# The first transfers chained by their landings, the first two pieces cut smaller, and TensorE multiplying a cleared tile at the start of a decoder layer

## The chip, the cores and the metric

One Trainium2 chip, one of its cores. The number that counts is the device time of one execution in microseconds (us), as the median of the runs. Lower is better. The engines of the core are TensorE (PE in the profile, its weight loads apart as PEld), VectorE (DVE), ScalarE (ACT), GpSimd (POOL) and SyncE (SP), which issues almost all transfers.

## The reference

One layer of a decoder for 256 tokens of width 2048, all float32. Every `x @ w` below is a dense product, and the weights are far larger than what is held on the chip, so they are streamed.

```python
def swiglu(x, w_gate, w_up, w_down):
    return (jax.nn.silu(x @ w_gate) * (x @ w_up)) @ w_down
...
h = swiglu(rms_norm(x, ffn1_pre_g), ffn1_w_gate, ffn1_w_up, ffn1_w_down)   # 2048 -> 5632 -> 2048
x = x + 0.5 * rms_norm(h, ffn1_post_g)
u = rms_norm(x, mix_pre_g)
c_q, c_kv, k_rope, q_m, k_m, v_m = jnp.split(u @ w_in, cuts, axis=-1)
a = mla_attention(c_q, c_kv, k_rope, ...)
m = moba_attention(q_m, k_m, v_m)
y = jnp.concatenate([rms_norm(a, mla_out_g), rms_norm(m, moba_out_g)], axis=-1) @ w_out
x = x + rms_norm(y, mix_post_g)
h = swiglu(rms_norm(x, ffn2_pre_g), ffn2_w_gate, ffn2_w_up, ffn2_w_down)
x = x + 0.5 * rms_norm(h, ffn2_post_g)
```

Only the beginning of the first SwiGLU matters here: the product of the scaled x with the gate and up weights.

## The kernel before

**The stream.** The host lays all weights out as a stream of pieces, each `[128, 2048]` float32, 1 MB. In the gate-and-up stage a piece holds four chunks of 512 columns (256 gate and 256 up columns, for 128 rows of the contraction). Four pieces, 16 chunks, make the contraction over 2048 for one block of 256 hidden columns. SyncE loads the pieces in order into four slots of `raw` (piece n into slot n mod 4), and may load piece n only when the piece four earlier has been split (`raw_free`, a wait on `lo_ready`).

**The split.** The products are made from pairs of reduced-precision numbers. ScalarE rounds a piece to `w_hi`, and VectorE makes `w_lo = raw - w_hi` (`take_high`, `take_low`; two slots each, so `take_high` of piece n waits for `piece_used`, that TensorE is done with piece n - 2). TensorE then makes three products per chunk and token tile (`three_passes`): hi by hi, hi by lo, lo by hi. A piece is 4 chunks x 2 token tiles x 3 = 24 matmuls of 128x512.

**The left operand.** For the first stage the host gives x also turned (`x_turned`), and the transfer brings it to `xT` in four quads of four chunks, 512 KB each. `turn_high` (ScalarE, L406) multiplies a chunk by the gain of its rows and rounds it to `act_hi`. `turn_low` (VectorE, L711) makes `act_lo`. Each is one 128x256 instruction per chunk. TensorE waits for `act_ready` of each chunk, and for `lo_ready` of each piece.

**The gains** come as 70 rows of 128 numbers into `gain_in`. TensorE turns them with `ident` (L1406), and ScalarE copies the result to `gain`. Before TensorE can begin it waits for `consts_made`, `gains_landed` and `gains_kept`.

**The order at the start.** SyncE issues without a wait: the first half of piece 0, xT quad 0, the second half of piece 0, then piece 1, quad 1, piece 2, quad 2, piece 3, quad 3. Then piece 4, the first half of `rows` (x itself, 1 MB), piece 5, the second half of `rows`, piece 6, piece 7, a gain row and a table. ScalarE's order is: half 0 of piece 0, the gains, quad 0 (four chunks), half 1 of piece 0, piece 1, quad 1, piece 2, quad 2, quad 3, piece 3, the square of `rows` tile 0, piece 4, the square of tile 1, piece 5. VectorE follows in the same order, with piece 3 last of the first four. TensorE goes through the pieces in order.

```python
for n in range(RAW):
    if n:
        load(piece(n))
    sp.dma_start(xT[:, 4 * n:4 * n + 4, :], xT_in[:, 4 * n:4 * n + 4, :]).then_inc(xT_landed[n], 16)
```

Of the kernel before, what the change touches and what calls it, by code (L numbers as in the profile page):

```python
# [25 lines left out]
P = 128  # L26
# [14 lines left out]
RAW = 4  # L41
PIECE = 2048
EPS = 1e-6
# [8 lines left out]
GU1 = 0  # L52
# [56 lines left out]
def build_layer(nc, x, xT_in, stream, gains, post_gains, rope, out):  # L109
    ctx = ExitStack()  # L110
    with ctx:
# [14 lines left out]
        gain_in = sb("gain_in", [G_ROWS, P])  # L126
# [62 lines left out]
        xT_landed = [sem(f"xT_landed{k}") for k in range(4)]  # L189
# [8 lines left out]
        gains_turned = sem("gains_turned")  # L198
        gains_kept = sem("gains_kept")
# [21 lines left out]
        first_landed = sem("first_landed")  # L221
        first_hi_ready = sem("first_hi_ready")
        first_lo_ready = sem("first_lo_ready")
# [58 lines left out]
        def _(sp):  # L282
# [20 lines left out]

            sp.dma_start(raw[:, 0, 0:PIECE // 2], stream[0, :, 0:PIECE // 2]).then_inc(first_landed, 16)
            for n in range(RAW):
                if n:
                    load(piece(n))
                sp.dma_start(xT[:, 4 * n:4 * n + 4, :], xT_in[:, 4 * n:4 * n + 4, :]).then_inc(xT_landed[n], 16)
                if n == 0:
                    sp.dma_start(raw[:, 0, PIECE // 2:], stream[0, :, PIECE // 2:]).then_inc(raw_landed[0], 16)  # L310
# [27 lines left out]
        def _(pool):  # L338
            nc.gpsimd.memset(ident[:, :], 0.0)
            nc.gpsimd.memset(mask[:, :], 0.0)  # L340
# [49 lines left out]
        def _(act):  # L390
# [7 lines left out]
            def turn_high(turn, k, chunks=range(4)):  # L398

                if turn == 0:  # L400
                    act.wait_ge(xT_landed[k], 16)
                else:
                    act.wait_ge(quad_turned, 4 * (turn - 1) + k + 1)
                for j in chunks:
# [29 lines left out]
            def gate_up(stage, turn):  # L434


                turn_high(turn, 0)
# [223 lines left out]
            def mix_out():  # L661
# [37 lines left out]
        def _(dve):  # L699
# [5 lines left out]
            def turn_low(turn, k, chunks=range(4)):  # L705

                for j in chunks:
                    c = 4 * k + j
                    if j % 2 == 0:
# [347 lines left out]
            def scale_out(n, t):  # L1057
# [6 lines left out]
            dve.wait_ge(first_hi_ready, 1)  # L1064
            nc.vector.tensor_tensor(w_lo[:, 0, 0:PIECE // 2], raw[:, 0, 0:PIECE // 2], w_hi[:, 0, 0:PIECE // 2],
                                    ALU.subtract).then_inc(first_lo_ready, 1)
            dve.wait_ge(gains_kept, 1)
            turn_low(0, 0)
            dve.wait_ge(hi_ready, 1)
            nc.vector.tensor_tensor(w_lo[:, 0, PIECE // 2:], raw[:, 0, PIECE // 2:], w_hi[:, 0, PIECE // 2:],  # L1070
                                    ALU.subtract).then_inc(lo_ready, 1)
            take_low(piece(GU1 + 1))
            turn_low(0, 1)
# [19 lines left out]
        def _(pe):  # L1093
# [23 lines left out]
            def dense_piece(pc, i, blk, parity, width=BANK, n_turn=None):  # L1117

                halves = isinstance(pc.index, int) and pc.index == 0
                if halves:  # L1120
                    pe.wait_ge(first_lo_ready, 1)
                else:
                    pe.wait_ge(lo_ready, pc.index + 1)
# [3 lines left out]
                for j in range(4):  # L1127
                    c = 4 * i + j
                    if halves and j == 2:
# [259 lines left out]
            def mix_out():  # L1389
# [93 lines left out]
```

## Time and profile before

| | |
|---|---|
| median of 3 runs | 1875.18 us (1874.47 to 1875.34) |
| profiled execution, own time | 1875.26 us |
| its span, first to last instruction | 1873.4 us |
| TensorE matmul busy | 1847.7 us, 99% of the span |
| weight loads, VectorE, ScalarE | 1496.7, 934.6, 798.7 us |
| mean granted TensorE clock | 0.997 |
| first matmul of the product | 7.79 us after the span's start |

The span is what the trace shows; the execution's own time is 1.86 us longer. TensorE is busy nearly always, so the other engines' totals say little: what matters is when TensorE first starts, and each moment at which it stands.

### The profile page before, as it was taken

How to read it: one execution, taken by the hardware profiler on the slowest of the kernel's cores; microseconds unless marked ns; L12 is line 12 of the kernel's file. 1: busy time of each engine (PE TensorE's matmuls, PEld its weight loads, DVE VectorE, ACT ScalarE, POOL GpSimd, SP SyncE). 2: the span in 40 equal slices, each digit the busy share in tenths (PEclk: the TensorE clock that was granted, in tenths of full speed). 3: DMA queues.
4: the chain of work that ended last, by engine and by line, in shares of the span. 5: the costliest groups of instructions: out<-in, count | busy, mean ns of one | idle time of the engine just before them, and what ended most of it. 6: DMA issues, size and time to landing. Idle time of an engine off the chain costs nothing.

```text
span 1873.4 us, 21527 instructions
## 1 busy us (share of the span) xinstructions
PE 1847.7 (99%) x8233; PEld 1496.7 (80%) x8233; DVE 934.6 (50%) x857; ACT 798.7 (43%) x791; POOL 27.4 (1%) x59
## 2 busy tenths in 40 slices
PE   8999999999999999999999999999999999999997
PEld 6888888888878888788888878888888888788886
DVE  5444444444455554655577464444444444445545
ACT  6333433334444444543347345443333333444443
POOL 0000000000000000000000000000000000000000
PEclk9999999999999999999999999999999999999999
DMA  9454554545445545365441555555455554555552
GB/s 366 180 182 183 190 184 179 179 186 186 185 182 180 194 186 182 137 221 182 170 152 69 180 182 181 184 189 185 179 181 186 190 182 179 179 183 197 180 189 103
DMA packets 49063, 341.09 MB, mean 182 GB/s; under 512 B 5438, under 2 KB 5764, under 8 KB 9092
## 3 DMA queue, kind: packets, MB, share of 16 engines
q1 hardware_dynamic: 48944, 340.58, 50.2%
q8 instruction: 23, 0.38, 0.1%
q14 instruction: 12, 0.10, 0.0%
q10 hardware_dynamic: 84, 0.04, 0.0%
HBM read 338.50 MB, written 2.10 MB: 182 GB/s over the span
## 4 chain that ended last, share of the span: by engine, by line
PE 97%; DVE 1%; ACT 1%; issue 0%; DMA 0%; DVEq 0%; POOL 0%; ACTq 0%
PE banks L1191 26%; PE banks L1098 23%; PE banks L1096 23%; PE banks L1097 22%; PE banks L1161 1%; PE banks L1113 1%; DVE rows L735 0%; PE banks L1320 0%; PE banks L1321 0%; PE banks L1331 0%; DMA raw<-in_weights 0%; ACT w_hi L478 0%; DVE scaled L786 0%; PE banks L1227 0%; DVE w_lo L702 0%
## 5 line engine op out<-in xcount | busy, mean ns | idle before, releaser
L702 DVE TENSOR_TENSOR w_lo<-raw,w_hi 128x2048 fp32r<-128x2048 f32 (+3 forms) x229 | 515.1, 2249 | 671.2 <-ACT w_hi L395 671.2
L395 ACT ACTIVATE w_hi<-raw 128x2048 fp32r<-128x2048 f32 (+3 forms) x229 | 431.0, 1882 | 757.0 <-PE banks L1098 752.3
L1096 PE MATMUL banks<-w_hi,act_hi 128*128 128x512 f32 (+1 forms) x1728 | 686.1, 397 | 3.7 <-DVE act_lo L711 2.8
L1098 PE MATMUL banks<-w_hi,act_lo 128*128 128x512 f32 (+1 forms) x1728 | 683.7, 396 | 0.0
L1097 PE MATMUL banks<-w_lo,act_hi 128*128 128x512 f32 (+1 forms) x1728 | 678.4, 393 | 0.0
L1096 PEld LDWEIGHTS banks<-w_hi,act_hi 128*128 128x128 f32 x1728 | 325.4, 188 | 78.0 <-issue 3.9
L1097 PEld LDWEIGHTS banks<-w_lo,act_hi 128*128 128x128 f32 x1728 | 325.5, 188 | 77.4
L1098 PEld LDWEIGHTS banks<-w_hi,act_lo 128*128 128x128 f32 x1728 | 325.1, 188 | 77.5
L1191 PE MATMUL banks<-w_hi,hid_split 128*128 128x512 f32 x1408 | 386.1, 395 | 0.0
L775 DVE TENSOR_TENSOR w_lo<-raw,w_hi 128x2048 fp32r<-128x2048 f32 x88 | 201.6, 2291 | 236.3 <-ACT w_hi L478 236.3
L1191 PEld LDWEIGHTS banks<-w_hi,hid_split 128*128 128x128 f32 x1408 | 264.0, 188 | 65.5 <-DVE hid_split L778 0.5
L478 ACT ACTIVATE w_hi<-raw 128x2048 fp32r<-128x2048 f32 x88 | 168.6, 1916 | 269.2 <-PE banks L1191 255.4
L1191 PE MATMUL banks<-w_lo,hid_split 128*128 128x512 f32 x704 | 221.5, 396 | 0.0
L1191 PEld LDWEIGHTS banks<-w_lo,hid_split 128*128 128x128 f32 x704 | 132.2, 188 | 31.0
L778 DVE TENSOR_TENSOR hid_split<-hidT,hid_split 128x512 fp32r<-128x512 f32 x88 | 60.1, 683 | 0.0
L479 ACT CAST hid_split<-hidT 128x512 fp32r (+1 forms) x88 | 52.8, 600 | 0.0
L722 DVE SCALAR_TENSOR_TENSOR hid<-banks,rs,silu 128x256 f32<-128x256 f32 x88 | 38.2, 476 | 0.0
L425 ACT ACTIVATE silu<-banks,rs 128x256 f32<-128x256 f32 x88 | 36.1, 461 | 0.0
L368 POOL TENSOR_SCALAR var<-sumsq 128x1 f32<-128x1 f32 x20 | 8.1, 403 | 1542.3 <-ACT junk L415 1316.6
L431 ACT COPY hidT<-banks 128x512 f32 (+1 forms) x44 | 25.0, 567 | 6.6 <-PE banks L1161 6.6
L1161 PEld LDWEIGHTS banks<-ident,hid 128*128 128x128 f32 x176 | 21.7, 140 | 7.1 <-issue 1.4
L1161 PE MATMUL banks<-ident,hid 128*128 128x128 f32 x176 | 26.4, 272 | 0.5 <-DVE hid L722 0.5
(119 smaller groups left out, 606.5 us busy)
## 6 DMA issues: line engine op xcount, KB each, us to landing
raw<-in_weights SPq DMA_DIRECT2D x307, 1024.0 KB, 4.8
raw<-in_weights SPq DMA_DIRECT2D x6, 512.0 KB, 3.8
gain_row<-in_post_gains SPq DMA_DIRECT2D x3, 1024.0 KB, 6.9
raw<-in_weights SPq DMA_DIRECT2D x4, 768.0 KB, 4.1
raw<-in_weights SPq DMA_DIRECT2D x4, 640.0 KB, 3.8
xT<-in_x_turned SPq DMA_DIRECT2D x4, 512.0 KB, 10.2
rows<-in_x SPq DMA_DIRECT2D x2, 1024.0 KB, 13.8
out_rows<-rows SPq DMA_DIRECT2D x8, 256.0 KB, 2.8
```

The lines of the kernel that those rows point to most:

```text
L395: nc.scalar.activation(w_hi[:, pc.split, 0:width], raw[:, pc.slot, 0:width], ACT.Copy)\
L478: nc.scalar.activation(w_hi[:, pc.split, :], raw[:, pc.slot, :], ACT.Copy).then_inc(hi_ready, 1)
L479: nc.scalar.copy(hid_split[:, pc.split, 0], hidT[:, bass.ds(2 * n, 2), :]).then_inc(hid_hi_ready, 1)
L702: nc.vector.tensor_tensor(w_lo[:, pc.split, 0:width], raw[:, pc.slot, 0:width], w_hi[:, pc.split, 0:width], ALU.subtract).then_inc(lo_read ...
L722: nc.vector.scalar_tensor_tensor(out=hid[:, t, :], in0=result(parity, t)[:, FB:], scalar=rs[:, job, t:t + 1], in1=silu[:, t, :], op0=ALU.m ...
L775: nc.vector.tensor_tensor(w_lo[:, pc.split, :], raw[:, pc.slot, :], w_hi[:, pc.split, :], ALU.subtract)
L778: nc.vector.tensor_tensor(hid_split[:, pc.split, 1], hidT[:, bass.ds(2 * n, 2), :], hid_split[:, pc.split, 0], ALU.subtract).then_inc(lo_r ...
L1096: nc.tensor.matmul(out_ap, hi, rhs_hi, start=start, stop=False, skip_group_check=chain)
L1097: nc.tensor.matmul(out_ap, hi, rhs_lo, start=False, stop=False, skip_group_check=chain)
L1098: return nc.tensor.matmul(out_ap, lo, rhs_hi, start=False, stop=stop, skip_group_check=chain)
L1161: mm = nc.tensor.transpose(banks[:, 4, c * TOKENS + t * P:c * TOKENS + (t + 1) * P], hid[:, t, tile_of(c)], ident[:, :])
L1191: mm = nc.tensor.matmul(banks[:, b + n, :], lhs, rhs[:, j, quarter(n)], start=first and j == 0 and lhs is hi and rhs is rhs_hi, stop=True, ...
```

## The change

Transfers: piece 0 comes in four quarters (chunks) and the first xT quad in two pairs of chunks. The first four transfers are issued at once. Quarter 2 waits for quarter 0 to have landed, quarter 3 for the first pair, piece 1 for quarter 1, xT quad 1 for quarter 3, piece 2 for piece 1, and piece 3 for piece 2. What stands behind a waiting transfer on SyncE's queue waits with it.

Split: piece 0 is rounded and subtracted by quarters, each followed by its one chunk of x. Piece 1 goes by halves, each followed by two chunks of x. TensorE waits for each of these parts.

Gains: the host gives them turned, `[128, 70]`, and they land in `gain` directly. TensorE's turn of them, ScalarE's copy and both waits are gone.

TensorE: after GpSimd has cleared `mask` (now its first instruction of its own) and before it waits for the constants, it makes 10 matmuls of the cleared tile by itself into a bank that nothing reads.

```diff
+WARM = 10
...
-            sp.dma_start(raw[:, 0, 0:PIECE // 2], stream[0, :, 0:PIECE // 2]).then_inc(first_landed, 16)
-            for n in range(RAW):
-                if n:
-                    load(piece(n))
-                sp.dma_start(xT[:, 4 * n:4 * n + 4, :], xT_in[:, 4 * n:4 * n + 4, :]).then_inc(xT_landed[n], 16)
-                if n == 0:
-                    sp.dma_start(raw[:, 0, PIECE // 2:], stream[0, :, PIECE // 2:]).then_inc(raw_landed[0], 16)
+            def load_chunk(j):
+                sp.dma_start(raw[:, 0, quarter(j)], stream[0, :, quarter(j)]).then_inc(chunk_landed[j], 16)
+
+            for j in range(2):
+                load_chunk(j)
+                sp.dma_start(xT[:, 2 * j:2 * j + 2, :], xT_in[:, 2 * j:2 * j + 2, :]).then_inc(xT_pair_landed[j], 16)
+            sp.wait_ge(chunk_landed[0], 16)
+            load_chunk(2)
+            sp.wait_ge(xT_pair_landed[0], 16)
+            load_chunk(3)
+            for n in range(1, RAW):
+                if n == 1:
+                    sp.wait_ge(chunk_landed[1], 16)
+                else:
+                    sp.wait_ge(raw_landed[n - 1], 16)
+                load(piece(n))
+                if n == 1:
+                    sp.wait_ge(chunk_landed[3], 16)
+                sp.dma_start(xT[:, 4 * n:4 * n + 4, :], xT_in[:, 4 * n:4 * n + 4, :]).then_inc(xT_landed[n - 1], 16)
...
+            nc.gpsimd.memset(mask[:, :], 0.0).then_inc(mask_cleared, 1)
             nc.gpsimd.memset(ident[:, :], 0.0)
-            nc.gpsimd.memset(mask[:, :], 0.0)
...
                 if turn == 0:
-                    act.wait_ge(raw_landed[0], 16)
-                    nc.scalar.activation(w_hi[:, 0, PIECE // 2:], raw[:, 0, PIECE // 2:], ACT.Copy)\
-                      .then_inc(hi_ready, 1)
-                    take_high(piece(stage + 1))
-                turn_high(turn, 1)
+                    for j in range(4):
+                        act.wait_ge(chunk_landed[j], 16)
+                        nc.scalar.activation(w_hi[:, 0, quarter(j)], raw[:, 0, quarter(j)], ACT.Copy)\
+                          .then_inc(chunk_hi_ready if j < 3 else hi_ready, 1)
+                        if j == 0:
+                            act.wait_ge(gains_landed, 16)
+                        if j % 2 == 0:
+                            act.wait_ge(xT_pair_landed[j // 2], 16)
+                        turn_high(turn, 0, (j,))
+                    act.wait_ge(raw_landed[1], 16)
+                    for half in range(2):
+                        cols = slice(half * PIECE // 2, (half + 1) * PIECE // 2)
+                        nc.scalar.activation(w_hi[:, 1, cols], raw[:, 1, cols], ACT.Copy)\
+                          .then_inc(hi_ready if half else chunk_hi_ready, 1)
+                        if half == 0:
+                            turn_high(turn, 1, (0, 1))
+                else:
+                    turn_high(turn, 0)
+                turn_high(turn, 1, range(4) if turn else (2, 3))
...
-            act.dma_start(gain_in[:, :], gains).then_inc(gains_landed, 16)
-            act.wait_ge(first_landed, 16)
-            nc.scalar.activation(w_hi[:, 0, 0:PIECE // 2], raw[:, 0, 0:PIECE // 2], ACT.Copy)\
-              .then_inc(first_hi_ready, 1)
-            act.wait_ge(gains_turned, 1)
-            nc.scalar.copy(gain[:, :], banks[:, 7, 256:256 + G_ROWS]).then_inc(gains_kept, 1)
-            act.wait_ge(gains_kept, 1)
+            act.dma_start(gain[:, :], gains).then_inc(gains_landed, 16)
...
+            for j in range(4):
+                if j < 3:
+                    dve.wait_ge(chunk_hi_ready, j + 1)
+                else:
+                    dve.wait_ge(hi_ready, 1)
+                nc.vector.tensor_tensor(w_lo[:, 0, quarter(j)], raw[:, 0, quarter(j)], w_hi[:, 0, quarter(j)],
+                                        ALU.subtract).then_inc(chunk_lo_ready if j < 3 else lo_ready, 1)
+                turn_low(0, 0, (j,))
+            for half in range(2):
...
+                nc.vector.tensor_tensor(w_lo[:, 1, cols], raw[:, 1, cols], w_hi[:, 1, cols],
+                                        ALU.subtract).then_inc(lo_ready if half else chunk_lo_ready, 1)
+                turn_low(0, 1, (2 * half, 2 * half + 1))
...
+                    if early == 0 and j < 3:
+                        pe.wait_ge(chunk_lo_ready, j + 1)
+                    elif early == 0:
                         pe.wait_ge(lo_ready, 1)
+                    elif early == 1 and j == 0:
+                        pe.wait_ge(chunk_lo_ready, 4)
+                    elif early == 1 and j == 2:
+                        pe.wait_ge(lo_ready, 2)
...
+            pe.wait_ge(mask_cleared, 1)
+            for _ in range(WARM):
+                nc.tensor.matmul(banks[:, 5, 0:P], mask[:, 0:P], mask[:, 0:P], start=True, stop=True)
             pe.wait_ge(consts_made, 1)
-            pe.wait_ge(gains_landed, 16)
-            nc.tensor.transpose(banks[:, 7, 256:256 + G_ROWS], gain_in[:, :], ident[0:G_ROWS, 0:G_ROWS])\
-              .then_inc(gains_turned, 1)
-            pe.wait_ge(gains_kept, 1)
             gate_up(GU1, 0)
```

## Rows read from the trace of the kernel before

**Rows 1.** The page's first part: busy time, share of the span, instructions.

```profile
PE 1847.7 (99%) x8233; PEld 1496.7 (80%) x8233; DVE 934.6 (50%) x857; ACT 798.7 (43%) x791; POOL 27.4 (1%) x59
```

**Rows 2.** The page's chain that ended last, its shares by engine.

```profile
PE 97%; DVE 1%; ACT 1%; issue 0%; DMA 0%; DVEq 0%; POOL 0%; ACTq 0%
```

**Rows 3.** Timeline, 0 to 27 us: start, us, engine, line, count, [idle before <-releaser].

```profile
1.17 0.42 SPq L308 DMA_DIRECT2D xT<-in_x_turned  x1
...
4.82 1.06 ACT L678 ACTIVATE w_hi<-raw 128x1024 fp32r<-128x1024 f32 x1 [2.12 <-DMA raw<-in_weights]
...
5.91 1.23 DVE L1065 TENSOR_TENSOR w_lo<-raw,w_hi 128x1024 fp32r<-128x1024 f32 x1 [5.91 <-ACT w_hi L678]
6.13 1.70 ACT L406 ACTIVATE act_hi<-xT,gain 128x256 fp32r<-128x256 f32 x4
7.16 1.67 DVE L711 SCALAR_TENSOR_TENSOR act_lo<-xT,gain,act_hi 128x256 fp32r<-128x256 f32 x4
...
7.79 0.77 PE L1096 MATMUL banks<-w_hi,act_hi 128*128 128x512 f32 x1 [2.84 <-DVE act_lo L711]
...
10.45 1.92 ACT L395 ACTIVATE w_hi<-raw 128x2048 fp32r<-128x2048 f32 x1 [1.47 <-DMA raw<-in_weights]
...
12.40 2.29 DVE L702 TENSOR_TENSOR w_lo<-raw,w_hi 128x2048 fp32r<-128x2048 f32 x1 [2.16 <-ACT w_hi L395]
...
15.23 0.47 PE L1096 MATMUL banks<-w_hi,act_hi 128*128 128x512 f32 x1
...
19.24 1.71 ACT L406 ACTIVATE act_hi<-xT,gain 128x256 fp32r<-128x256 f32 x4 [0.33 <-DMA xT<-in_x_turned]
...
20.91 0.39 PE L1096 MATMUL banks<-w_hi,act_hi 128*128 128x512 f32 x1
...
21.17 1.92 ACT L395 ACTIVATE w_hi<-raw 128x2048 fp32r<-128x2048 f32 x1 [0.23 <-PE banks L1098]
...
23.12 2.29 DVE L702 TENSOR_TENSOR w_lo<-raw,w_hi 128x2048 fp32r<-128x2048 f32 x1 [0.32 <-ACT w_hi L395]
...
24.21 1.92 ACT L415 ACTIVATE junk<-rows 128x2048 bf16<-128x2048 f32 x1 [1.12 <-DMA rows<-in_x]
...
26.51 0.39 PE L1096 MATMUL banks<-w_hi,act_hi 128*128 128x512 f32 x1
```

**Rows 4.** DMA issues, 1.1 to 1.6 us: KB, us from issue to landing.

```profile
xT<-in_x_turned SPq DMA_DIRECT2D x1, 512.0 KB, 4.9
```

**Rows 5.** The page's DMA issues, whole span: count, KB, median us to landing.

```profile
raw<-in_weights SPq DMA_DIRECT2D x307, 1024.0 KB, 4.8
raw<-in_weights SPq DMA_DIRECT2D x6, 512.0 KB, 3.8
```

**Rows 6.** The tile raw, 60 to 400 us (59 loads of 1 MB).

```profile
DMA to landing us min/median/max: 4.6/4.8/6.0
```

**Rows 7.** Windows: us, busy (x) of PE, PEld, DVE, ACT, POOL, granted clock, DMA share, GB/s.

```profile
7.79:11.34 3.55, 3.55 (x8) 2.78 (x9) 2.27 (x4) 1.99 (x3) 0.00 (x0) 1.00 1.01 422
11.34:14.89 3.55, 3.55 (x16) 2.87 (x15) 2.49 (x2) 2.62 (x5) 0.00 (x0) 1.00 1.02 425
...
759.00:766.00 7.00, 4.34 (x20) 3.53 (x19) 5.58 (x10) 5.03 (x9) 0.81 (x2) 0.76 0.26 94
...
1111.10:1115.00 3.90, 3.89 (x11) 3.14 (x12) 3.90 (x6) 1.60 (x5) 0.00 (x0) 0.63 0.76 315
```

**Rows 8.** Timeline of PE, places inside the kernel where it stood.

```profile
762.60 2.82 PE L1113 MATMUL banks<-ident,rows 128*128 128x128 f32 x12 [1.88 <-DVE rows L735]
...
983.45 0.55 PE L1331 MATMUL banks<-ident,probs 128*128 128x128 f32 x3 [1.01 <-ACT probs L617]
983.84 0.39 PE L1341 MATMUL banks<-v,probsT 128*128 128x128 f32 x2
984.06 0.39 PE L1342 MATMUL banks<-v,probsT 128*128 128x128 f32 x2
...
1108.91 2.18 PE L1113 MATMUL banks<-ident,rows 128*128 128x128 f32 x12 [1.56 <-DVE rows L735]
```

More of the change, by code:

```diff
@@ L125, in build_layer @@
         mask = sb("mask", [P, 2 * P])
-        gain_in = sb("gain_in", [G_ROWS, P])
         gain = sb("gain", [P, G_ROWS])
@@ L186, in build_layer @@
         banks = ctx.enter_context(nc.psum_tensor("banks", [P, 8, BANK], F32))
-        xT_landed = [sem(f"xT_landed{k}") for k in range(4)]
+        xT_landed = [sem(f"xT_landed{k}") for k in range(1, 4)]
         rows_landed = [sem(f"rows_landed{t}") for t in range(TILES)]
@@ L197, in build_layer @@
         consts_made = sem("consts_made")
-        gains_turned = sem("gains_turned")
-        gains_kept = sem("gains_kept")
+        mask_cleared = sem("mask_cleared")
         hi_ready = sem("hi_ready")
@@ L220, in build_layer @@
         lat_ready = sem("lat_ready")
-        first_landed = sem("first_landed")
-        first_hi_ready = sem("first_hi_ready")
-        first_lo_ready = sem("first_lo_ready")
+        chunk_landed = [sem(f"chunk_landed{j}") for j in range(3)] + [raw_landed[0]]
+        xT_pair_landed = [sem(f"xT_pair_landed{j}") for j in range(2)]
+        chunk_hi_ready = sem("chunk_hi_ready")
+        chunk_lo_ready = sem("chunk_lo_ready")
         y_scaled = sem("y_scaled")
@@ L398, in turn_high @@
             def turn_high(turn, k, chunks=range(4)):
-                if turn == 0:
-                    act.wait_ge(xT_landed[k], 16)
-                else:
+                if turn:
                     act.wait_ge(quad_turned, 4 * (turn - 1) + k + 1)
+                elif k:
+                    act.wait_ge(xT_landed[k - 1], 16)
                 for j in chunks:
@@ L434, in gate_up @@
             def gate_up(stage, turn):
-                turn_high(turn, 0)
                 if turn == 0:
-                    act.wait_ge(raw_landed[0], 16)
-                    nc.scalar.activation(w_hi[:, 0, PIECE // 2:], raw[:, 0, PIECE // 2:], ACT.Copy)\
-                      .then_inc(hi_ready, 1)
-                    take_high(piece(stage + 1))
-                turn_high(turn, 1)
+                    for j in range(4):
[17 more added lines that the diff above has]
+                turn_high(turn, 1, range(4) if turn else (2, 3))
                 take_high(piece(stage + 2))
@@ L708, in turn_low @@
                     c = 4 * k + j
-                    if j % 2 == 0:
+                    if turn == 0 and k == 0:
+                        dve.wait_ge(act_hi_ready, j + 1)
+                    elif j % 2 == 0:
                         dve.wait_ge(act_hi_ready, DC * turn + c + 2)
@@ L1061, in scale_out @@
                                         ALU.mult).then_inc(y_scaled, 1)
[L1064 to L1073, printed above, removed]
+            for j in range(4):
[7 more added lines that the diff above has]
+            for half in range(2):
+                cols = slice(half * PIECE // 2, (half + 1) * PIECE // 2)
+                if half == 0:
+                    dve.wait_ge(chunk_hi_ready, 4)
+                else:
+                    dve.wait_ge(hi_ready, 2)
+                nc.vector.tensor_tensor(w_lo[:, 1, cols], raw[:, 1, cols], w_hi[:, 1, cols],
+                                        ALU.subtract).then_inc(lo_ready if half else chunk_lo_ready, 1)
+                turn_low(0, 1, (2 * half, 2 * half + 1))
             take_low(piece(GU1 + 2))
@@ L1117, in dense_piece @@
             def dense_piece(pc, i, blk, parity, width=BANK, n_turn=None):
[L1119 to L1122, printed above, removed]
+                early = pc.index if isinstance(pc.index, int) and pc.index < 2 else None
+                if early is None:
                     pe.wait_ge(lo_ready, pc.index + 1)
@@ L1128, in dense_piece @@
                     c = 4 * i + j
-                    if halves and j == 2:
+                    if early == 0 and j < 3:
+                        pe.wait_ge(chunk_lo_ready, j + 1)
+                    elif early == 0:
                         pe.wait_ge(lo_ready, 1)
+                    elif early == 1 and j == 0:
+                        pe.wait_ge(chunk_lo_ready, 4)
+                    elif early == 1 and j == 2:
+                        pe.wait_ge(lo_ready, 2)
                     if n_turn is not None:
@@ L1472 @@
         "weights": lay_out_weights(w),
-        "gains": np.concatenate(gains).reshape(G_ROWS, P),
+        "gains": np.ascontiguousarray(np.concatenate(gains).reshape(G_ROWS, P).T),
         "post_gains": np.concatenate([w["ffn1_post_g"], w["mix_post_g"], w["ffn2_post_g"]]),
```

## The prediction

> **What bounds the kernel now.** I read the page's busy times first, then the chain, then the timeline of the first 30 us. TensorE is busy 1847.7 of 1873.4 us [rows 1] and holds 97% of the chain that ended last [rows 2]. So a change at the start is worth exactly what it moves the point from which TensorE no longer stands; all after that point shifts with it. The reader should find that point first, and it isn't the first matmul.
>
> The start before, from [rows 3]: the first half of piece 0 lands at 4.8 us, ScalarE and VectorE work, and the first matmul starts at 7.79. Piece 1 starts at 15.23, piece 2 at 20.91, piece 3 at 26.51: 5.6 us apart, 24 matmuls at 0.233 us. The first 8 matmuls take 3.55 us and the next 16 take another 3.55 [rows 7], 0.44 against 0.22 each: TensorE begins at 1.2 GHz and rises to 2.4 GHz at about 11.3 (the clock column says 1.00 for both, so here the count has to be read, not the column). After 15.23 TensorE does not stand for a long time.
>
> But the supply is close behind. Piece 3 needs the last quad of xT, which lands at 19.24 (ScalarE stood for it [rows 3]). Then come, on ScalarE, 1.71 us for the quad and 1.92 for piece 3's w_hi, and on VectorE 2.29 for its w_lo, each started within 0.03 of the last: 5.95 us in all, so piece 3 could start at 19.24 + 5.95 = 25.2. It started at 26.51. Only 1.3 us of a gain in front of it can be kept, even if no transfer is later than now.
>
> **Transfers, the part that decides.** Before, nine transfers lie in the queue at once, and landings follow the bytes: 512 KB at 4.8, the next 512 KB at 1.17 + 4.9 = 6.07 [rows 3, 4], so 0.63 us per 256 KB; the 1 MB rows that land at 24.2 end 2 MB that follow the last quad, 2.5 us per MB [rows 3]. A transfer issued only when another has landed pays its full way: 4.8 us median for 1 MB, 3.8 for 512 KB [rows 5], bounds 4.6 and 6.0 [rows 6]. For 256 KB no row exists; the two medians continued give 3.3. Bounds: 2.9 (4.8 less 0.75 MB at 2.5 us per MB) and 3.8; I take 3.3, the nearer to the 512 KB row.
>
> The first four (1 MB) are issued as before: quarter 0 at about 4.2 (4.8 less 0.63), pair 0 at 4.8, quarter 1 at 5.45, pair 1 at 6.07. Quarter 2 is issued at 4.25 and lands at 7.55; quarter 3 at 4.85, lands 8.15. Piece 1 is issued at 5.5: 10.3 by the median, and by bytes it ends the same 2.5 MB as before, 10.45 [rows 3]; I take 10.45. Quad 1 follows it by 1.25: 11.7. Piece 2 is issued at 10.5 and lands at 15.3. Piece 3 is issued at 15.35 and lands at 20.15; quad 3, queued behind it, at 21.4. That is 2.15 later than the 19.24 of before. Everything queued behind on SyncE (piece 4, rows, piece 5) is as much later.
>
> By the Trainium skill, "DMA: Bandwidth & Descriptors", section "Anatomy of one DMA", a transfer has a fixed 2.0 us besides its bytes at 436 GB/s, mostly the receipt of the last byte, and its rules for kernel authors say to issue early and wait late; this speaks against the change. By its formula 1 MB would be an estimated 4.4 us instead of the measured 4.8, and the sum below 0.8 us smaller.
>
> **The first pieces.** A quarter of w_hi is 0.63 us (from 1.06 for half and 1.92 for a whole), a quarter of w_lo 0.70 (from 1.23 and 2.29), one chunk of x 0.42 to 0.5 on each engine [rows 3]. Chunk 0: w_hi 4.2 to 4.85, act_hi to 5.3, w_lo to 5.55, act_lo to 6.05, first matmul 6.1 instead of 7.79: 1.7 us earlier. The gains' own row is gone from this chain: no turn, no copy. They come now as 128 short rows instead of 70; should they land after 4.85, the first matmul is that much later, which the gap before piece 1 (below) covers up to 1 us. Chunks 1 to 3 are ready at 7.25, 9.35 and 10.5, a chunk takes 1.4 us at full clock, so piece 0 is done at 12.2.
>
> Piece 1: w_hi of its first half 10.45 to 11.5, w_lo to 12.75, act_hi of two chunks 11.7 to 12.55, act_lo of the first to 13.2. TensorE starts it at 13.25, after 1.05 us of standing, 2.0 earlier than before. The second half is ready at 15.35, needed at 16.05. Done at 18.9. Piece 2 (landed 15.3): w_hi to 17.2, w_lo to 19.5, act_lo to 19.95, start 20.0 after 1.1 us of standing; 0.9 earlier than before. Done at 25.65. Piece 3: 21.4 + 5.95 = 27.35, after 1.7 us of standing; 0.85 **later** than the 26.51 of before, and 0.9 with the slower first matmul after a stand (0.08, as at 15.23).
>
> Behind it: rows tile 0 lands 4.97 after quad 3 as before, 26.35; the square (1.92, and some 0.2 to read its sum, an estimate), w_hi and w_lo of piece 4 end at 32.65, while TensorE ends piece 3 at 33.0. That covers it by 0.35 us, whatever the landing, since both follow quad 3. From there nothing stands and the 0.9 stays to the end. The later stalls [rows 8] shift with it.
>
> **The cleared tile.** A float32 matmul of 128 columns shows as two records, 0.22 us at full clock from 983.84 to 984.06 [rows 8], so 0.44 at half: 10 cost 4.4 us. What covers them is the wait for chunk 0 until 6.1: begun before 1.7 us, which one memset ahead of them should allow, they cost nothing; if they ran past the cover, the first matmul would be later and again the gap before piece 1 would take it. Gain, if they raise the clock: 8 x 0.2 = 1.6 us in piece 0. But piece 1 waits for data until 13.25. Without any rise, piece 0 would end at 6.1 + 3.55 + 16 x 0.233 = 13.4; piece 1 starts 0.15 later, and piece 2's stand swallows that. So this part is worth 0 at the end, with bounds 0 and 1.6.
>
> **Sum.** Against the profiled execution's 1875.26: +0.9. The median shown is 0.08 below it, so 1875.18 + 0.9 = 1876.1 us.
>
> **Rivals.**
> Clock falls (0.22). Inside the kernel TensorE stood 1.88 us and 1.56 us [rows 8], and in both places the granted clock fell to 1.2 GHz for a while: a mean of 0.76 over 7 us and 0.63 over 3.9 us [rows 7], 3.4 and 2.9 us at half. After a stand of 1.01 the spacing stayed at full clock (two 128-column records in 0.22) [rows 8]. My stands are 1.05, 1.1 and 1.7. A fall before piece 1 or 2 is taken up by the next stand; one before piece 3 isn't: 8 matmuls at 0.2 more, +1.6, in all +2.5: 1877.7. The two rows with falls were among short transposes, not dense matmuls, which speaks against. The Trainium skill, "TensorE: Matmul & The Clock Gate", section "HAM oscillation", says the same of bursts parted by waits for data; the 1.56 row agrees. This is the rival on the other side of no change: with hops near 6.0 us (+2.4) it would be +4.9, and it decides from a hop of about 5.4 on.
> Waits cost nothing (0.22): the chained transfers land no later than now. For: the queue still holds a quad behind each piece. Then piece 3 starts at 25.2 + 0.08: 1.25 earlier, 1873.9.
> Hops much longer (0.05): slower by 3.75 needs quad 3 at 24.2, both hops at 6.2 us; 6.0 is the longest of 59. About 1879.
> Supply faster than now (0.05): bytes land 0.6 us or more earlier since fewer transfers share the engines, all gains at the start kept: start 1.7, clock 1.6 and the stand from 14.89 to 15.23 [rows 3, 7] of 0.35, 3.65 and so 1871.5 at the very most; about 1872.5 for most of it.
> The forecast itself (0.46), with hops of 4.6 to 5.2: own range 1875.6 to 1876.9.
>
> **Numbers.** A measurement of this kernel can tell about 0.2%, 3.75 us, from no change. The largest gain is 3.65, so faster by more has 0.02; slower by more needs the long hops, or a fallen clock with middling ones: 0.07; same 0.91. The range 1873.8 to 1878.2 takes in the forecast, the fallen clock and the free waits, and leaves out the two ends and a part of the middle ones.
>
> **What would show it.** Right: first matmul near 6.1; three stands of TensorE before pieces 1, 2 and 3, released by VectorE; piece 2 and 3 landing 4.8 after issue; quad 3 near 21.4; DMA share with holes where it was 1.0; piece 3 starting at 27.3. Half-clock spacing after the last stand shows the first rival. Wrong: if quad 3 lands before 20.6, the sum turns to a gain; if the spacing in piece 0 is 0.44 the tile did nothing, and the end shouldn't move by it.

## The result

The changed kernel takes 1881.73 us (median of 7 runs, 1878.82 to 1883.17), the kernel before 1874.73 (7 runs, 1874.21 to 1875.34). The ratio is 1.0033, with a 95% interval of 1.0023 to 1.0043: slower by 0.33%, 7.0 us between the two medians. The forecast was no change, 1876.1 us, with a range up to 1878.2. The runs of the changed kernel also scatter over 4.4 us where those of before scatter over 1.1. One execution in all that follows took 9123.58 us, one of the seven of the run with quad 1 behind piece 1's landing; it is left out of that run's ratio.

The page of the changed kernel, its busy times and its chain by engine. Beside [rows 1] and [rows 2]: TensorE is 6.7 us longer busy, of which 4.6 us are the matmuls of the cleared tile, and transfers now have 1% of the chain.

```profile
PE 1854.4 (99%) x8252; PEld 1501.7 (80%) x8252; DVE 935.3 (50%) x860; ACT 799.2 (43%) x793; POOL 27.5 (1%) x59
...
PE 96%; DVE 1%; DMA 1%; ACT 1%; issue 0%; SPq 0%; DVEq 0%; POOL 0%; ACTq 0%
```

The timeline of the changed kernel, columns as in [rows 3], put in order of time. SPq L290 issues pieces, SPq L322 quads of xT.

```profile
1.09 4.64 PE L1438 MATMUL banks<-mask 128*128 128x128 f32 x20 [1.09 <-POOL mask L351]
...
5.93 0.33 SPq L290 DMA_DIRECT2D raw<-in_weights  x1
6.52 0.76 PE L1124 MATMUL banks<-w_hi,act_hi 128*128 128x512 f32 x1 [0.79 <-DVE act_lo L732]
...
9.73 0.33 SPq L322 DMA_DIRECT2D xT<-in_x_turned  x1
...
12.21 0.33 SPq L290 DMA_DIRECT2D raw<-in_weights  x1
12.22 1.06 ACT L462 ACTIVATE w_hi<-raw 128x1024 fp32r<-128x1024 f32 x1 [1.45 <-DMA raw<-in_weights]
...
14.60 0.91 ACT L418 ACTIVATE act_hi<-xT,gain 128x256 fp32r<-128x256 f32 x2 [1.33 <-DMA xT<-in_x_turned]
16.17 0.47 PE L1124 MATMUL banks<-w_hi,act_hi 128*128 128x512 f32 x1 [2.27 <-DVE act_lo L732]
19.64 1.91 ACT L407 ACTIVATE w_hi<-raw 128x2048 fp32r<-128x2048 f32 x1 [2.39 <-DMA raw<-in_weights]
...
24.42 0.47 PE L1124 MATMUL banks<-w_hi,act_hi 128*128 128x512 f32 x1 [0.87 <-DVE act_lo L732]
26.36 1.71 ACT L418 ACTIVATE act_hi<-xT,gain 128x256 fp32r<-128x256 f32 x4 [3.21 <-DMA xT<-in_x_turned]
27.98 1.90 ACT L407 ACTIVATE w_hi<-raw 128x2048 fp32r<-128x2048 f32 x1
29.91 2.29 DVE L721 TENSOR_TENSOR w_lo<-raw,w_hi 128x2048 fp32r<-128x2048 f32 x1 [0.93 <-ACT w_hi L407]
32.26 0.50 PE L1124 MATMUL banks<-w_hi,act_hi 128*128 128x512 f32 x1 [2.00 <-DVE w_lo L721]
```

Read it from the bottom. Piece 3 starts at 32.26, where it started at 26.51 [rows 3]: 5.75 us later. Above it stands the chain of quad 3: landed at 26.34, then 1.7 + 1.9 + 2.3 us of work, 5.9 in all. So quad 3's landing is what moved, from 19.24 to 26.34. Further up are the hops (a hop is the time of one transfer from its issue to its landing): piece 1 issued at 5.93 and landed at 12.2 (6.3 us), piece 2 issued at 12.21 and landed at 19.6 (7.4 us), and quad 1 issued at 9.73 only, for it waits for quarter 3, and landed at 14.6 (4.9 us).

The windows of the changed kernel, columns as in [rows 7]; the last one lies in piece 3.

```profile
6.00:8.00 2.00, 1.48 (x4) 1.22 (x5) 1.46 (x3) 0.97 (x2) 0.00 (x0) 1.00 0.62 179
...
12.00:14.00 2.00, 1.91 (x9) 1.20 (x7) 0.69 (x1) 1.06 (x1) 0.00 (x0) 1.00 0.88 225
...
18.00:19.60 1.60, 1.60 (x5) 1.28 (x4) 0.50 (x2) 0.00 (x0) 0.00 (x0) 0.50 0.07 31
...
33.80:37.20 3.40, 3.40 (x10) 2.66 (x9) 2.03 (x1) 1.34 (x1) 0.46 (x1) 0.50 1.00 424
```

The kernel before, the same three stretches of the start (the last two columns are the share of the transfer engines and GB/s).

```profile
6.00:8.00 2.00, 0.21 (x1) 0.24 (x2) 1.98 (x4) 1.78 (x5) 0.00 (x0) 1.00 0.98 352
...
12.00:14.00 2.00, 2.00 (x11) 1.59 (x10) 1.60 (x1) 1.96 (x5) 0.00 (x0) 1.00 0.99 412
...
18.00:19.60 1.60, 1.60 (x9) 1.28 (x8) 1.60 (x2) 1.27 (x4) 0.00 (x0) 1.00 1.06 438
```

There are the holes: 179 GB/s instead of 352, 225 instead of 412, and before piece 2 lands 1.6 us at 31 GB/s and a share of 0.07. That is one of the 16 transfer engines: the trace has a landing event for each engine's part of piece 2, and fifteen of them come between 16.65 and 17.28, the sixteenth at 19.62. All that time SyncE holds back the next piece. And the granted clock falls to half after the stand of 2.0 us, 1.5 us after piece 3 has started: 3.4 us at 0.50, some 8 matmuls at 0.43 instead of 0.233, 1.55 us that nothing takes up. 5.75 + 1.55 = 7.3 us. The copies of the hidden columns bear it out: from 53 to 526 us each of them stands 7.4 us later than before, so nothing more is lost there and the steady part keeps its pace. After 1156 us they stand 6.5 us later, as much as the span grew: of the two later falls of the clock in [rows 7], the one near 1111 us does not occur in this execution.

### The profile page after: what moved, and what is told of

It is laid out like the page before. It is cut to its first block, busy times and chain, and to the rows that moved or that the text cites. A ratio compares the mean times of both kernels' runs of the same rounds, so it can differ in the third digit from the quotient of the medians.

```text
span 1879.9 us, 21574 instructions
## 1 busy us (share of the span) xinstructions
PE 1854.4 (99%) x8252; PEld 1501.7 (80%) x8252; DVE 935.3 (50%) x860; ACT 799.2 (43%) x793; POOL 27.5 (1%) x59
## 4 chain that ended last, share of the span: by engine, by line
PE 96%; DVE 1%; DMA 1%; ACT 1%; issue 0%; SPq 0%; DVEq 0%; POOL 0%; ACTq 0%
PE banks L1223 25%; PE banks L1126 22%; PE banks L1124 22%; PE banks L1125 22%; PE banks L1193 1%; DMA raw<-in_weights 1%; PE banks L1141 1%; DVE rows L756 0%; DMA xT<-in_x_turned 0%; DVE w_lo L721 0%; PE banks L1352 0%; PE banks L1353 0%; PE banks L1363 0%; ACT w_hi L503 0%; ACT w_hi L407 0%
```

## The experiments

Times are medians, each beside the kernel before on the same chip (1874.94 to 1875.01 in every group). "Quad 3" is the moment at which its first act_hi starts after standing for the transfer; it is read from the one profiled execution, while the time is the median of all. A shorter way to say where a run stands: piece 3 starts 5.9 us after quad 3, unless TensorE is later.

**All waits out.**

```diff
-            sp.wait_ge(chunk_landed[0], 16)
             load_chunk(2)
-            sp.wait_ge(xT_pair_landed[0], 16)
             load_chunk(3)
             for n in range(1, RAW):
-                if n == 1:
-                    sp.wait_ge(chunk_landed[1], 16)
-                else:
-                    sp.wait_ge(raw_landed[n - 1], 16)
                 load(piece(n))
-                if n == 1:
-                    sp.wait_ge(chunk_landed[3], 16)
```

> The changed kernel with all of SyncE's waits for landings at the start taken out; sizes and order of the transfers stay. Theory A (the chained waits make each transfer pay its whole way, which the queue otherwise hides): quad 3 of xT lands near 19.3 us instead of 26.3, the stand before piece 3 shrinks from 2.0 us to under 0.5, the time is 1872.5 to 1874.5. Theory B (the small first transfers are what is slow: they put back everything behind them): quad 3 still lands after 22 us, time over 1876.5. Theory C (the clock that falls after TensorE's stands is most of the loss): only 1.5 us less than the changed kernel, about 1880.

1874.62 us, ratio to the kernel before 0.9999 (0.9990 to 1.0008). The whole loss, 7.1 us, is the waits'. The timeline of this run:

```profile
6.37 0.48 PE L1116 MATMUL banks<-w_hi,act_hi 128*128 128x512 f32 x1 [0.64 <-DVE act_lo L724]
...
20.85 1.71 ACT L410 ACTIVATE act_hi<-xT,gain 128x256 fp32r<-128x256 f32 x4 [1.47 <-DMA xT<-in_x_turned]
...
26.74 0.50 PE L1116 MATMUL banks<-w_hi,act_hi 128*128 128x512 f32 x1 [0.25 <-DVE w_lo L713]
```

Its window from 6 to 8 us, where before has 352 GB/s and the changed kernel 179:

```profile
6.00:8.00 2.00, 1.63 (x7) 1.37 (x8) 1.31 (x3) 0.85 (x2) 0.00 (x0) 1.00 0.90 271
```

TensorE begins 1.4 us earlier than before and here at full clock, and piece 3 still starts at 26.74: quad 3 landed at 20.8, 1.6 later than before, though nothing waits. Theory A is right in that the waits make the loss, but its figures (quad 3 near 19.3, at most 1874.5 us) are missed by little: something else eats the rest of the gain. Note piece 1, which lands at 12.07 here, hardly earlier than the 12.2 of the changed kernel.

**Only the early waits.** The same edit for pieces 2 and 3 alone.

> The changed kernel without the waits of piece 2 for piece 1 and of piece 3 for piece 2; the four waits on quarters and the first pair stay. Theory A: the two long hops (7.4 and 4.8 us from issue to landing) carry most of the loss; piece 2 and 3 land by bytes behind piece 1, which landed at 12.2 against 10.4, so quad 3 lands at about 21 and the time is 1875 to 1877. Theory B: over 1878.

1878.59 us (1875.07 to 1880.72), 1.0016 (1.0007 to 1.0025); quad 3 at 23.83. Theory A's figure of 1875 to 1877 was too low. By the medians, taking out the last two waits gains 3.1 us and the early waits carry 4.0 (this run's own times scatter over 5.7 us). The reason shows in the queue: quad 1 still waits for quarter 3, so it and all behind it are issued from 9.81 on only.

**No cleared tile.** The loop of ten matmuls taken out.

> The changed kernel without the ten matmuls of the cleared tile. In the changed kernel the first real matmuls are 0.43 us apart all the same, until 3.4 us after they begin. Theory A: no difference to the changed kernel beyond 1 us, 1879 to 1883, since a later piece waits for its transfer anyway. Theory C: if the cleared tile does change the clock's course (where it falls and rises), the time moves by 1.5 us or more.

1880.84 us (1877.63 to 1882.08), 1.0027 (1.0016 to 1.0038), quad 3 at 25.66. The interval overlaps that of the changed kernel. No worth of the tile shows at the end, as the forecast had it.

**The kernel before with only the two late waits.**

```diff
                 if n:
+                    if n > 1:
+                        sp.wait_ge(raw_landed[n - 1], 16)
                     load(piece(n))
```

> The kernel before with only two waits added: piece 2 is issued when piece 1 has landed, piece 3 when piece 2 has. Theory A: piece 1 lands at 10.4 as before, two hops of 4.8 to 7.4 follow, quad 3 lands at 21.4 to 25, time 1876 to 1881. Theory B: within 1 us of the kernel before, 1874 to 1876.

1876.01 us (1875.28 to 1876.89), 1.0006 (0.9997 to 1.0015). The timeline of this run:

```profile
10.42 1.91 ACT L397 ACTIVATE w_hi<-raw 128x2048 fp32r<-128x2048 f32 x1 [1.50 <-DMA raw<-in_weights]
...
15.35 0.33 SPq L290 DMA_DIRECT2D raw<-in_weights  x1
...
21.82 1.71 ACT L408 ACTIVATE act_hi<-xT,gain 128x256 fp32r<-128x256 f32 x4 [2.87 <-DMA xT<-in_x_turned]
...
27.71 0.50 PE L1098 MATMUL banks<-w_hi,act_hi 128*128 128x512 f32 x1 [1.06 <-DVE w_lo L704]
```

This is the forecast's own chain, almost to the tenth: piece 1 at 10.4, one hop of 4.9, quad 3 at 21.8 (forecast 21.4), piece 3 at 27.71 (27.35), +1.0 us (+0.9). The arithmetic of the late hops was right; what goes before them in the changed kernel was not.

**Large first transfers, no waits.** Half, quad and half as before; ScalarE's waits adapted, the work by quarters kept.

```diff
-            for j in range(2):
-                load_chunk(j)
-                sp.dma_start(xT[:, 2 * j:2 * j + 2, :], ...)
-            load_chunk(2)
-            load_chunk(3)
+            sp.dma_start(raw[:, 0, 0:PIECE // 2], ...).then_inc(chunk_landed[1], 16)
+            sp.dma_start(xT[:, 0:4, :], ...).then_inc(xT_pair_landed[0], 16)
+            sp.dma_start(raw[:, 0, PIECE // 2:], ...).then_inc(chunk_landed[3], 16)
```

> The changed kernel without SyncE's waits and with the first transfers in the sizes of before (half, quad, half), while ScalarE, VectorE and TensorE still go by quarters; the gains come turned, the cleared tile stays. Without waits but with small transfers piece 1 landed at 12.1 and quad 3 at 20.8 us, against 10.45 and 19.24 before. Theory B2 (the 256 KB transfers with their 2 KB rows move the same bytes more slowly, some 1.6 us in all): piece 1 at 10.4, quad 3 near 19.3, piece 3 starts near 25.3, time 1873 to 1874. Theory G (the gains, now 128 rows of 280 bytes instead of 70 of 512, are what is slow): piece 1 still near 12, quad 3 near 20.8, time 1874.6 as without waits.

1874.52 us, 0.9997 (0.9988 to 1.0006). Piece 1 at 11.28, quad 3 at 20.59, against 12.07 and 20.85 with the small ones. Neither theory's figures hold: the sizes account for 0.8 us at piece 1 and little at quad 3.

**Gains in 512-byte rows, no waits, small transfers.** The host pads the turned gains to `[128, 128]`.

> The changed kernel without SyncE's waits, with the turned gains padded by the host to 128 rows of 512 bytes; the small transfers stay. Theory G: piece 1 lands near 10.5, quad 3 near 19.3, time about 1873.5. Theory B2: as without waits, piece 1 near 12.1, quad 3 near 20.8, time within 0.5 us of 1874.6.

1870.52 us, 0.9973 (0.9962 to 0.9985): lower than either theory, with quad 3 at 20.11 and piece 3 at 26.01. Only 0.7 us lie there. The rest lies in the steady part, 22.75 us per block of hidden columns instead of 22.84: the padding had also shifted every tile that is allocated later. The two things had to be parted (below).

**Quad 1 not waiting.** The changed kernel without the one wait on `chunk_landed[3]`.

> The changed kernel with one wait taken out: quad 1 of xT no longer waits for quarter 3 but is issued right behind piece 1. Theory Q (piece 2's hop of 7.4 us is long because quad 1, issued at 9.7, is still in flight when piece 2 is issued at 12.2): piece 2's hop falls to about 5, quad 3 lands 1.5 to 2.5 us earlier than 26.3, time 1.5 to 2.5 us less than the changed kernel's, 1879 to 1880. Theory S (a single lagging transfer engine makes the hop long, whatever lies behind it): quad 3 near 25.5 to 26.5, time 1880.5 to 1882.5.

1879.07 us, 1.0023 (1.0013 to 1.0033), 2.7 below the changed kernel. The timeline of this run:

```profile
12.37 0.33 SPq L290 DMA_DIRECT2D raw<-in_weights  x1
...
17.09 1.91 ACT L405 ACTIVATE w_hi<-raw 128x2048 fp32r<-128x2048 f32 x1 [0.82 <-DMA raw<-in_weights]
...
23.58 1.71 ACT L416 ACTIVATE act_hi<-xT,gain 128x256 fp32r<-128x256 f32 x4 [2.97 <-DMA xT<-in_x_turned]
...
29.47 0.50 PE L1122 MATMUL banks<-w_hi,act_hi 128*128 128x512 f32 x1 [1.75 <-DVE w_lo L719]
```

Piece 2's hop is 4.7 instead of 7.4, quad 3 2.8 us earlier and the time 2.7 us less: theory Q, by a little more than it said. In the four traces that keep this wait, the chain and the small transfers (the changed kernel, the one without the cleared tile, the one with padded gains, the shifted one) the hop of piece 2 is 6.5 to 7.4. So this one wait makes the hop long.

**The kernel before with the whole chain of waits**, large transfers kept.

```diff
                 if n:
+                    sp.wait_ge(xT_landed[0] if n == 1 else raw_landed[n - 1], 16)
                     load(piece(n))
+                if n == 1:
+                    sp.wait_ge(raw_landed[0], 16)
                 sp.dma_start(xT[:, 4 * n:4 * n + 4, :], ...)
                 if n == 0:
+                    sp.wait_ge(first_landed, 16)
                     sp.dma_start(raw[:, 0, PIECE // 2:], ...)
```

> The kernel before, large first transfers and all, with the whole chain of waits: second half for first half, piece 1 for quad 0, quad 1 for the second half, piece 2 for piece 1, piece 3 for piece 2. Theory A (waits alone, whatever the sizes): hops of 4.8 to 5: second half lands near 8.9, piece 1 at 11 to 12, quad 1 near 13, piece 2 at 16.5, quad 3 at 22.8 to 23.5, time 1877 to 1878. Theory B2 (waits and small transfers each have a part): this one stays 3 us or more below the changed kernel's 1881.7. Theory A2 (the early waits are what cost, sizes do nothing): quad 3 at 25 or later, time 1879 to 1882.

1879.06 us (1877.51 to 1880.47), 1.0021 (1.0012 to 1.0030). The timeline of this run:

```profile
6.22 0.33 SPq L290 DMA_DIRECT2D raw<-in_weights  x1
...
13.62 1.92 ACT L399 ACTIVATE w_hi<-raw 128x2048 fp32r<-128x2048 f32 x1 [3.87 <-DMA raw<-in_weights]
...
25.20 1.71 ACT L410 ACTIVATE act_hi<-xT,gain 128x256 fp32r<-128x256 f32 x4 [3.18 <-DMA xT<-in_x_turned]
```

So large transfers do not save a chain: piece 1 takes 7.4 us here. Landing and time are both where A2 put them, at the low end. Quad 1 waits too, but lands only 1.3 us after piece 1 (14.87), and piece 2's hop behind it is 4.9. B2's mark, 3 us or more below the changed kernel, is missed by little at 2.7, so a small part of the sizes isn't excluded.

**Place in memory.** The kernel before with one unused tile (32 bytes per partition) behind `gain`, nothing else.

```diff
         gain = sb("gain", [P, G_ROWS])
+        sb("shift_by", [P, 8])
```

> The kernel before with one unused tile of 32 bytes per partition allocated behind gain: everything allocated later, act_hi, act_lo and hid_split among it, then starts at a multiple of 64 bytes instead of 32 past one. Nothing else differs. Theory P (place in memory: the 0.09 us per block of hidden columns by which the run with padded gains was quicker in its steady part comes from this shift, which the padding brought about): 22.75 instead of 22.84 us per block, time near 1871. Theory G2 (it is the gains' rows in some way): no change, 1875.

1843.20 us (1841.81 to 1844.54), 0.9833 (0.9819 to 0.9846). The place does it, and by far more than either theory gave.

Gains in 512-byte rows without waits, with the later tiles put back to their old place:

> The changed kernel without SyncE's waits, gains in 128 rows of 512 bytes, and the same unused tile of 32 bytes, which here puts the later tiles back to 32 past a multiple of 64, as in the kernel before. It compares with the run without waits (1874.6, quad 3 at 20.85) in the gains' rows alone. Theory P: 22.84 us per block; the time is 1873.5 to 1874.6, by what the rows move quad 3 (20.1 to 20.8). Theory G2: near 1870.5 as with the padded gains before.

1874.87 us, 0.9999 (0.9990 to 1.0008), quad 3 at 20.09. With the old place the padded gains are worth 0.8 us at quad 3's landing and nothing in the time. The gain of the run with padded gains was the place alone (1870.52 there, 1874.87 here).

Large first transfers as well:

> No waits, the large first transfers, gains in 512-byte rows, later tiles at multiples of 64; ScalarE, VectorE and TensorE by quarters, cleared tile kept. Quad 3 near 19.3 us as before, piece 3 starts near 25.2 to 25.5 instead of 26.5, and by theory P 0.09 us less per block: 1869 to 1870. If the small transfers were no cost: 1870.5 as with them.

1869.82 us, 0.9972 (0.9960 to 0.9983), piece 1 at 10.54, quad 3 at 19.17: the supply is as before again. Both the small transfers and the short gain rows had cost at the start. The time is that of the other place.

The changed kernel, waits and all, with padded gains at the old place:

> The changed kernel with all its waits, gains in 512-byte rows, and the unused 32 bytes so that later tiles lie as in the changed kernel (32 past a multiple of 64). Theory R (the short rows of the gains load the transfer engines at the start, and a chain of waits multiplies this): quad 3 lands at 23 to 25 instead of 26.3, time 1878.5 to 1880.5. Theory A (the waits and the late quad 1 do it): quad 3 within 0.7 us of 26.3, time 1880.5 to 1882.

1882.46 us (1879.14 to 1883.28), 1.0037 (1.0024 to 1.0051), quad 3 at 26.57. Theory R falls: taking the short rows out gives the changed kernel nothing back. But at piece 1 the pair with padded gains shows the early waits by themselves: 12.49 here, 11.30 without waits.

**Quad 1 behind piece 1's landing.**

> The changed kernel with quad 1 of xT waiting for piece 1's landing instead of quarter 3's, so that it is never issued while piece 1 is under way; piece 2 stands right behind it on the queue. Theory M (piece 2's hop of 7.4 us, with a single engine finishing 1.5 us after the others, comes from a transfer issued in the middle of another): no such tail, quad 1 lands near 16, piece 2 near 18.3, piece 3 at 23.2, quad 3 near 24.6, time about 1880. Theory T (the tail belongs to piece 2 whatever goes before): piece 2 lands at 19.5 or later, quad 3 at 26 or later, time 1881.5 or more.

1880.79 us, 1.0031 (1.0019 to 1.0043). Quad 1 was issued at 12.73 and landed at 17.3, 4.6 us for 512 KB where 3.8 is the median; piece 2, behind it, landed at 19.75 and quad 3 at 26.43. Theory M's landings fail and theory T's hold; the time, 1880.79, is between M's "about 1880" and T's 1881.5. No single engine lags here (piece 2's sixteen parts land from 18.7 to 19.73), so the long hop does not need one. Quad 1 is slow by itself: none of piece 2's packets starts before 15.5, and quad 1's own packets of 4 KB take 0.2 to 0.4 us on average, against 0.16 for most in the changed kernel. Why stays open.

**More places.** The changed kernel shifted, the kernel before by two more distances, and the best front (the start of the run with large first transfers, padded gains and no waits) at two places.

> The no-wait kernel with large first transfers and 512-byte gain rows, and 64 unused bytes behind gain, so that act_hi and what follows lie 64 past a multiple of 128, as in the shifted kernel before (1843.2). Theory P2 (place modulo 128 decides): 22.42 us per block, and 1 to 1.5 us from quad 3 at 19.2 and a front without waits: 1841 to 1843. Theory P3 (something finer than the place modulo 128): anything between 1843 and 1870.

1842.65 us, 0.9826 (0.9813 to 0.9839), as theory P2 had it.

> The kernel before with 96 unused bytes behind gain: later tiles at multiples of 128 instead of 64 past one. Theory P2: as with the padded gains, 22.75 us or more per block, 1869 to 1872. If a multiple of 64 is all that counts: 1843.

1828.80 us (1828.42 to 1829.00), 0.9753 (0.9741 to 0.9766). Neither expectation: lower than both. It isn't the place modulo 128.

> The changed kernel whole, with 32 unused bytes behind gain: later tiles 64 past a multiple of 512, as in the shifted kernel before. Theory P2: the steady part gains the same 31.8 us, and the start loses the same 6.7: about 1850. If place and waits interact (the tail of the transfers depends on where they write), it is off that by more than 2 us.

1849.94 us (1847.21 to 1850.73), 0.9862 (0.9848 to 0.9876), quad 3 at 27.04. 6.7 us above the shifted kernel before: the change costs about the same at another place (7.0 at the old one), so its loss is at the start, and no interaction of waits and place shows.

> The no-wait kernel with large first transfers and 512-byte gain rows, and 384 unused bytes behind gain, so that act_hi and what follows lie where they do in the best kernel so far (act_hi at byte 114816, 1828.8 us). Place alone: 22.24 us per block and the same time, 1828 to 1829.5. With the front worth anything more (quad 3 at 19.2, first matmul earlier): down to 1827.

1827.51 us (1827.03 to 1828.47), 0.9747 (0.9734 to 0.9761), the lowest of all; the front would be worth 1.3 us beside the 1828.80, but the intervals overlap, so it isn't shown.

> The kernel before with 160 unused bytes behind gain: act_hi at byte 114880, 192 past a multiple of 256. So far, by bytes past a multiple of 256: 0 gives 1870, 32 gives 1875, 64 gives 1843, 128 gives 1828.8. If the time depends on the distance from 128 alike on both sides: 1843. If each step away from 32 is better: below 1828.

1874.92 us, 0.9999 (0.9990 to 1.0009). Both expectations fail: the gain is gone again.

## Why the prediction was wrong

Point by point, by its own steps.

**What bounds the kernel: right.** The first moment from which TensorE no longer stands decides, and it is piece 3's start. In eight kernels at the old place the time follows quad 3: 19.24 (before, 1874.7), 20.85 (no waits, 1874.6), 21.82 (two late waits, 1876.0), 23.58 (quad 1 free, 1879.1), 23.83 (early waits, 1878.6), 25.20 (all chained, large, 1879.1), 25.66 (no cleared tile, 1880.8), 26.36 (changed, 1881.7). Up to about 20.8 nothing is lost, since TensorE reaches piece 3 at 26.5 anyway; from 21.82 to 25.20 some 0.9 us are lost per us (3.1 for 3.4), and beyond that 2.7 more for the next 1.2: in the traces the clock falls within piece 3 in the changed kernel and in the one without the cleared tile, and in none of the others of this list. A fall costs those other 1.5 us.

**Earlier first matmul: right.** 6.1 forecast, 6.52 measured. It does not reach the end: TensorE stood three times, as forecast, but pieces 1, 2 and 3 started at 16.17, 24.42 and 32.26 where 13.25, 20.0 and 27.35 were forecast.

**The late hops: right in themselves.** 4.8 to 4.9 us in the run with only these two waits, and +1.0 us where +0.9 was forecast. Of piece 3 in the changed kernel too (19.64 to about 24.5).

**The step that failed** is the one before: "by bytes it ends the same 2.5 MB as before, 10.45", and from it "Quad 1 follows it by 1.25: 11.7" and "Piece 2 is issued at 10.5 and lands at 15.3". The forecast put each early transfer's own way beside the byte rate of the full queue and took the larger.

First, piece 1 landed at 12.2, +1.75. The first four transfers landed 0.4 to 0.5 later than forecast, the two chained quarters took 4.0 and 4.4 us where 3.3 stood (its bounds were 2.9 and 3.8), and piece 1, issued at 5.93, took 6.3. The transfers moved 179 GB/s from 6 to 8 us, so the byte rate was not that of before. But the waits are only one cause of this: without any wait, and with 271 GB/s in that window, piece 1 landed at 12.07. There it was the small transfers and the short gain rows (10.54 with both undone). The forecast put both at nothing for piece 1's landing.

Second, quad 1 was counted as queued right behind piece 1, but its wait for quarter 3 holds it until 9.73. It landed at 14.6, +2.9, and 2.4 after piece 1 instead of 1.25. Piece 2 is issued at 12.21 while it is still under way, and its hop is 7.4 instead of 4.8. In the nine traces with chained pieces, every chained 1 MB took 4.6 to 5.0 us where the transfer before it in the queue landed within 1.3 us of its issue, and 6.3 to 7.4 us where that took 1.8 us or more. The forecast had the first kind only. With the wait on quad 1 gone the hop of piece 2 was 4.7.

The sums: +1.75 (piece 1), +2.6 (hop of piece 2), +0.6 (quad 3 follows piece 3 by 1.9 instead of 1.25) is +4.95, and quad 3 landed 4.95 later than the forecast's 21.4.

**The clock.** The rival "clock falls" had the mechanism and the place: after the stand before piece 3, 3.4 us at half, 1.55 us (forecast 1.6). An earlier fall, in piece 1, was taken up by the next stand, as forecast. The Trainium skill, "TensorE: Matmul & The Clock Gate", section "HAM oscillation", tells of bursts of matmuls that start slow after each wait for data. The trace agrees only in part: the clock did fall after a wait, but piece 3 began at full clock and lost it 1.5 us later, and the waits there are longer than the 2.0 us here. The rival's turning point was right as well: it needed its two hops at 5.4 us or more, and those of pieces 2 and 3 were 7.4 and 4.8, 6.1 on average. With hops near 6.0 it gave +4.9, the nearest of all the forecast's figures to the 7.0.

**The bound on hops** was the error in the range: 6.0 us was the longest of 59 loads that each ran alone [rows 6]. Hops that begin while an earlier transfer still has 1.8 us or more to go are another kind, and no row of before showed one. The chance for long hops, 0.05, was read from the wrong population. Nor was it one unlucky execution: the lowest of the seven runs, 1878.82, is above the range.

**The formula of the Trainium skill** ("DMA: Bandwidth & Descriptors", section "Anatomy of one DMA") is stated there for transfers that GpSimd issues, and these are SyncE's. The estimate of 4.4 us for 1 MB from it would have been further off than the row. The advice of that page's rules for kernel authors, to issue a transfer early and wait for it late, points the way in which the run without waits came out, 7.1 us.

**What stays open.** Why a single transfer engine ends piece 2 2.3 us after the others in the changed kernel (17.28 and 19.62) and in the one with padded gains (17.30 and 19.65). Without it the hop would have been 5.1. But in the kernel without the cleared tile and in the shifted one no engine lags by more than 0.4 us, and the hops are 6.5 and 7.2 all the same. Open too is why quad 1 takes 4.9 us in the changed kernel and 4.6 where it is issued behind piece 1's landing, when 3.8 is the median of 512 KB. That the late wait on quad 1 makes piece 2's hop long is shown; how, is not.

## What to carry to other kernels

In these runs a queue that was kept full landed 1 MB every 2.5 us, while a chained 1 MB took 4.6 us at the least and up to 7.4 where an earlier transfer was still under way. So price a chain from a run with that chain, not from transfers in another setting, and look at every transfer that a wait holds back with it. At the start of a kernel look for the first piece at which the slowest engine never stands again, and count only what reaches it. Before a difference of some tenths of a per cent is put down to an edit, check that the edit hasn't moved later tiles in memory: here an unused tile of 96 bytes per partition was worth 46 us, and all the waits together 7.

## What the runs showed of the hardware

**Where tiles lie sets TensorE's pace.** The copies of the hidden columns, 20 blocks apart. The kernel before:

```profile
45.39 0.56 ACT L431 COPY hidT<-banks 128x512 f32<-128x512 f32 x1
...
502.11 0.57 ACT L431 COPY hidT<-banks 128x512 f32 x1
```

The same kernel with 32 unused bytes per partition:

```profile
44.99 0.56 ACT L432 COPY hidT<-banks 128x512 f32<-128x512 f32 x1
...
493.35 0.56 ACT L432 COPY hidT<-banks 128x512 f32 x1
```

And with 96:

```profile
45.55 0.57 ACT L432 COPY hidT<-banks 128x512 f32<-128x512 f32 x1
...
490.35 0.56 ACT L432 COPY hidT<-banks 128x512 f32 x1
```

456.7, 448.4 and 444.8 us for 20 blocks: 22.84, 22.42 and 22.24 each. It is the matmuls: between 100 and 480 us nine tenths of the 128x512 matmuls start 230 to 238 ns after the one before, 225 to 232 with 32 bytes, and 226 to 231 with 96, 227 on average against 233. All tiles behind `gain` shift together (`act_hi`, `act_lo`, `hid_split` and `xT` among them), while `raw`, `w_hi` and `w_lo` stay at byte 128 past a multiple of 256 (the places are counted from the tiles' sizes; no trace shows them). The change itself takes out `gain_in`, 512 bytes, and so leaves the place past a multiple of 256 as it was. By the bytes of `act_hi` past a multiple of 256, the times are: at 0: 1870.52 and 1869.82 (both with fronts without waits); 32: 1874.7 (before) and, at another multiple, 1874.87; 64: 1843.20, and 1842.65 at another multiple with such a front; 128: 1828.80, and 1827.51 with such a front; 192: 1874.92. The time neither rises nor falls evenly with the distance, and which tile and which access make it was not tried.

**The cleared tile raises the clock in some executions only.** Ten matmuls of zeros from 1.09 to 5.7 us left the first real ones at half clock in the changed kernel's execution (first record 0.76 us) and at full clock in the run without waits (0.48). In the 13 traces with these matmuls the first real one is at full clock in 6 and at half in 7. All four with large first transfers, where TensorE stood 1.7 to 2.7 us after the cleared tile, are among the 7.

**The clock fell after a stand of 2.0 us between dense matmuls**, as it had among the transposes of [rows 8], and came back 3.4 us later. The same happened after stands of 1.98 to 2.17 us before piece 3 in three other runs (no cleared tile; padded gains at the old place; shifted by 32), and not after the 1.75 us in the run with quad 1 not waiting.
